# Side-by-side activation words: five matmuls per FFN weight tile instead of six

## The reference

```
for i in range(DEPTH):                      # DEPTH = 2
    x = x + 0.5 * _swiglu(_rmsnorm(x, norm_g[i, 0]), ffn_gu[i, 0], ffn_down[i, 0])
    x = x + mixer(_rmsnorm(x, norm_g[i, 1]))
    x = x + 0.5 * _swiglu(_rmsnorm(x, norm_g[i, 2]), ffn_gu[i, 1], ffn_down[i, 1])
return _rmsnorm(x, final_g), states

def _swiglu(x, w_gu, w_down):
    a, b = jnp.split(x @ w_gu, 2, axis=-1)  # 1024 -> 2 x 2816
    return (jax.nn.silu(a) * b) @ w_down    # 2816 -> 1024
```

## Time and profile before

| | |
|---|---|
| device time, median of 3 runs | 2866.24 us (2864.13 to 2870.95) |
| span of the profiled execution | 2867.4 us |
| the profiled execution's own time | not shown beside its span |
| TensorE matmuls busy | 2731.1 us, 95%, 21041 instructions |
| VectorE / ScalarE / GpSimd busy | 1276.3 us, 45% / 796.0 us, 28% / 285.8 us, 10% |
| one gate_up phase after its first tiles | 1414.9 to 1664.9 us, 250.0 us |
| one down phase | 1281.1 to 1409.5 us, 128.4 us |
| mean granted TensorE clock | 0.966 of 2.4 GHz |

### The profile page before, as it was taken

One profiled execution on the slowest core, in us unless ns is written; L12 is line 12 of the kernel. 1 busy time (PEld: TensorE's weight loads), 2 busy tenths in 40 slices (PEclk: granted clock), 3 DMA queues, 4 the chain that ended last, 5 costly groups with the idle time before them and its releaser, 6 DMA issues.

```text
span 2867.4 us, 49452 instructions
## 1 busy us (share of the span) xinstructions
PE 2731.1 (95%) x21041; PEld 2598.7 (91%) x21041; DVE 1276.3 (45%) x1563; ACT 796.0 (28%) x935; POOL 285.8 (10%) x299
## 2 busy tenths in 40 slices
PE   7999999999999999999999999899889888999997
PEld 6999997989888899999999999788878887999997
DVE  5444233435353454432344423565546654544323
ACT  3222222223231442222322222332223222322222
POOL 1000010101010110000100001003410242100000
PEclk9999999999999999999999999998989898999999
DMA  4333233515152333323433323220012100233231
GB/s 119 88 88 89 82 110 107 166 61 186 60 173 75 125 89 88 97 76 91 114 89 88 83 81 100 77 76 16 30 65 70 51 30 19 74 88 88 84 91 61
DMA packets 340931, 246.85 MB, mean 86 GB/s; under 512 B 9501, under 2 KB 322005, under 8 KB 340801
## 3 DMA queue, kind: packets, MB, share of 16 engines
q1 hardware_dynamic: 326480, 197.32, 23.5%
q0 software_dynamic: 14320, 47.61, 5.1%
HBM read 218.84 MB, written 26.05 MB: 85 GB/s over the span
## 4 chain that ended last, share of the span: by engine, by line
PE 88%; DVE 7%; issue 3%; ACT 2%; DMA 0%; SPq 0%; POOLq 0%; POOL 0%; DVEq 0%; ACTq 0%
PE ps L673 57%; PE ps L850 13%; PE ps L1010 6%; PE ps L771 2%; PE ps L743 1%; DVE cv L1678 1%; PE ps L761 1%; ACT wh L1150 1%; PE ps L749 1%; PE ps L710 1%; DVE wl L1401 1%; PE ps L961 1%; PE ps L968 0%; PE ps L1064 0%; PE ps L973 0%
## 5 line engine op out<-in xcount | busy, mean ns | idle before, releaser
L1401 DVE TENSOR_TENSOR wl<-raw,wh 128x2048 fp32r<-128x2048 f32 (+1 forms) x204 | 427.6, 2096 | 403.3 <-ACT wh L1150 403.3
L673 PE MATMUL ps<-xh,wh 128*128 128x260 f32 x2816 | 569.6, 283 | 4.7 <-DVE gate L1851 4.5
L673 PE MATMUL ps<-xh,wl 128*128 128x260 f32 x2816 | 568.7, 284 | 0.0
L673 PE MATMUL ps<-xl,wh 128*128 128x260 f32 x2816 | 567.9, 283 | 0.0
L1150 ACT ACTIVATE wh<-raw 128x2048 fp32r<-128x2048 f32 (+1 forms) x204 | 354.3, 1737 | 356.8 <-PE ps L673 223.2
L673 PEld LDWEIGHTS ps<-xh,wh 128*128 128x128 f32 x2816 | 436.0, 189 | 6.3 <-issue 5.2
L673 PEld LDWEIGHTS ps<-xh,wl 128*128 128x128 f32 x2816 | 435.5, 189 | 0.0
L673 PEld LDWEIGHTS ps<-xl,wh 128*128 128x128 f32 x2816 | 434.3, 189 | 0.0
L673 PE MATMUL ps<-hh,wh 128*128 128x260 f32 x1408 | 286.9, 285 | 13.4 <-DVE hl L1856 13.4
L673 PE MATMUL ps<-hh,wl 128*128 128x260 f32 x1408 | 284.9, 284 | 0.0
L673 PE MATMUL ps<-hl,wh 128*128 128x260 f32 x1408 | 284.8, 284 | 0.0
(11 more groups left out here) (315 smaller groups left out, 3047.7 us busy)
## 6 DMA issues: line engine op xcount, KB each, us to landing
raw<-in_ffn_gu_dram SPq DMA_DIRECT2D x176, 512.0 KB, 4.9
raw<-in_ffn_down_dram SPq DMA_DIRECT2D x64, 384.0 KB, 3.5
raw<-in_ret_w_in_dram SPq DMA_DIRECT2D x48, 512.0 KB, 4.3
raw<-in_ffn_down_dram SPq DMA_DIRECT2D x64, 320.0 KB, 4.0
s_ring<-in_state_ret_dram POOLq DMA_DIRECT2D x32, 512.0 KB, 4.5
out_dram<-s_ring POOLq DMA_DIRECT2D x32, 512.0 KB, 5.0
raw<-in_gdn_w_in_dram SPq DMA_DIRECT2D x32, 512.0 KB, 4.8
raw<-in_ret_w_out_dram SPq DMA_DIRECT2D x16, 512.0 KB, 4.3
```

The costliest lines, as they stand in the source:

```text
L673: m_ = nc.tensor.matmul(ps[:, 2 * q + h, 0:HALF], w_, v[:, kt0 + t, h * HALF:(h + 1) * HALF], start=b_, stop=e_)
L1401: nc.vector.tensor_tensor(wl[:, s, 0:cols], raw[:, s, 0:cols], wh[:, s, 0:cols].bitcast(F32), ALU.subtract).then_inc(w_low, 1)
```

## The change

In the FFN phases the high and low activation words of a tile lie side by side in one row of 2 x 520 words: first half's 260 high words and its first 86 low words (346), the same for the second half (346), then the remaining 174 low words of both halves (348). A high weight tile then takes three matmuls of 346, 346 and 348 columns; a low one two of 260 as before, on the high words. The low products no longer fall on the columns of the high ones: 2 x 86 columns lie beside them in the unit's two banks, and 348 in a third bank, 4 + u % 2. So evacuation has to add two parts.

- gate_up: ScalarE copies the low part out of PSUM into sq (two copies), VectorE adds it to the main part (this frees the unit) and then multiplies by rinv. The low words of h are written in two pieces.
- down: x gets the main part and then the low part in two pieces.
- The x tiles for gate_up phases (norms 0, 2, 3, 5) have the wide layout, made in two low pieces; those for the mixers and for the last norm stay as they were, in the same memory.
- Start: the sample tokens' transposes stand ahead of the loop, in bank 5, with one copy; the prompt's use banks 6 and 7.

```diff
 SLOT = 16 * P
+LA = 86
+LB = HALF - LA
+WA = HALF + LA
+WIDE = (0, 2, 3, 5)
 
 
...
+        xh = xm[:, 0:KT * NTOK].rearrange("p (t n) -> p t n", t=KT)
+        xl = xm[:, KT * NTOK:2 * KT * NTOK].rearrange("p (t n) -> p t n", t=KT)
+        xw = xm[:].rearrange("p (t n) -> p t n", t=KT)
+
+        def wide_high(tile):
+            return tile[:, 0:2 * WA].rearrange("p (h t) -> p h t", h=2)[:, :, 0:HALF]
+
+        def wide_low(tile):
+            return (tile[:, 0:2 * WA].rearrange("p (h t) -> p h t", h=2)[:, :, HALF:WA],
+                    tile[:, 2 * WA:2 * NTOK].rearrange("p (h t) -> p h t", h=2))
+
+        def pair_low(u):
+            return (ps[:, 2 * (u % 2):2 * (u % 2) + 2, HALF:WA],
+                    ps[:, 4 + u % 2, 0:2 * LB].rearrange("p (h t) -> p h t", h=2))
+
+        def tokens_low(ap):
+            t = halves(ap)
+            return t[:, :, 0:LA], t[:, :, LA:HALF]
...
+                nc.tensor.transpose(ps[:, 5, t * DEC:(t + 1) * DEC], xin_s[:, t * P:(t + 1) * P], ident[0:DEC, 0:DEC])
+            for t in range(KT):
                 if t >= 2:
                     pe.wait_ge(acc_free, t - 1)
-                b = 4 + 2 * (t % 2)
                 if t == 1:
                     pe.wait_ge(gains_ready, 1)
                 for c in range(4):
-                    nc.tensor.transpose(ps[:, b, c * P:(c + 1) * P], xin[:, c, t * P:(t + 1) * P], ident[:])
-                nc.tensor.transpose(ps[:, b + 1, 0:DEC], xin_s[:, t * P:(t + 1) * P],
-                                    ident[0:DEC, 0:DEC]).then_inc(parts_done, 1)
+                    m_ = nc.tensor.transpose(ps[:, 6 + t % 2, c * P:(c + 1) * P], xin[:, c, t * P:(t + 1) * P], ident[:])
+                m_.then_inc(parts_done, 1)
...
+            def wide_products(q, s, n_tiles, col0, tiles, kt0, first, last_):
+
+                for t in range(n_tiles):
+                    c = col0 + t * P
+                    hi_w, lo_w, v = wh[:, s, c:c + P], wl[:, s, c:c + P], tiles[:, kt0 + t]
+                    begin, end = first and t == 0, last_ and t == n_tiles - 1
+                    for h in range(2):
+                        nc.tensor.matmul(ps[:, 2 * q + h, 0:WA], hi_w, v[:, h * WA:(h + 1) * WA], start=begin, stop=False)
+                    nc.tensor.matmul(ps[:, 4 + q, 0:2 * LB], hi_w, v[:, 2 * WA:2 * NTOK], start=begin, stop=end)
+                    for h in range(2):
+                        m_ = nc.tensor.matmul(ps[:, 2 * q + h, 0:HALF], lo_w, v[:, h * WA:h * WA + HALF], start=False, stop=end)
                 return m_
...
-                                        m_ = products(g, s, 1, g * KT * P + t * P, P, xh, xl, t, t == 0, t == KT - 1)
+                                        m_ = wide_products(g, s, 1, g * KT * P + t * P, xw, t, t == 0, t == KT - 1)
...
-                                m_ = products(q, s, 11, 0, P, hh, hl, 11 * s, s == 0, s == 1)
+                                m_ = wide_products(q, s, 11, 0, hw, 11 * s, s == 0, s == 1)
...
-                            act.wait_ge(acc_free, ph.unit0 + 2 * j + 1)
-                            nc.scalar.activation(gate[:], gate[:], ACT.Silu).then_inc(gate_ready, 1)
+                            for g in range(2):
+                                act.wait_ge(parts_done, ph.unit_done(ph.unit0 + 2 * j + g))
+                                low = tokens_low(sq[:, g, :])
+                                nc.scalar.activation(low[0], pair_low(g)[0], ACT.Copy)
+                                nc.scalar.activation(low[1], pair_low(g)[1], ACT.Copy).then_inc(low_moved, 1)
+                                if g == 0:
+                                    act.wait_ge(gu_scaled, 2 * n + 1)
+                                    nc.scalar.activation(gate[:], gate[:], ACT.Silu).then_inc(gate_ready, 1)
                             act.wait_ge(h_ready, n + 1)
                             act.sem_inc(act_held, 1)
-                            nc.scalar.activation(hh[:, j, :], up[:], ACT.Copy).then_inc(h_high, 1)
+                            nc.scalar.activation(wide_high(hw[:, j]), halves(up[:]), ACT.Copy).then_inc(h_high, 1)
                     rolled(act, ph.slots // 2, body, True)
...
+                            high = wide_high(xw[:, t]) if ph.norm in WIDE else halves(xh[:, t, :])
+                            nc.scalar.activation(high, halves(x[:, t, :]), ACT.Copy,
...
+                gain = gains[:, bass.ds(KT * m + t, 1)]
+                if m not in WIDE:
+                    nc.vector.scalar_tensor_tensor(xl[:, t, :], x[:, t, :], gain, xh[:, t, :].bitcast(F32),
+                                                   ALU.mult, ALU.subtract).then_inc(x_low, 1)
+                    return
+                high, low, mine = wide_high(xw[:, t]).bitcast(F32), wide_low(xw[:, t]), tokens_low(x[:, t, :])
+                nc.vector.scalar_tensor_tensor(low[0], mine[0], gain, high[:, :, 0:LA], ALU.mult, ALU.subtract)
+                nc.vector.scalar_tensor_tensor(low[1], mine[1], gain, high[:, :, LA:HALF], ALU.mult, ALU.subtract).then_inc(x_low, 1)
...
-                                dve.wait_ge(parts_done, ph.unit_done(ph.unit0 + 2 * j + g))
-                                nc.vector.tensor_tensor(halves(t_[:]), pair(g), halves(rinv[:]), ALU.mult).then_inc(acc_free, 1)
+                                dve.wait_ge(low_moved, 2 * n + g + 1)
+                                nc.vector.tensor_tensor(halves(t_[:]), pair(g), halves(sq[:, g, :]), ALU.add).then_inc(acc_free, 1)
+                                dve.wait_ge(acc_free, ph.unit0 + 2 * j + g + 1)
+                                nc.vector.tensor_tensor(t_[:], t_[:], rinv[:], ALU.mult).then_inc(gu_scaled, 1)
                             dve.wait_ge(gate_ready, n + 1)
-                            dve.wait_ge(acc_free, ph.unit0 + 2 * j + 2)
+                            dve.wait_ge(gu_scaled, 2 * n + 2)
                             nc.vector.tensor_tensor(up[:], up[:], gate[:], ALU.mult).then_inc(h_ready, 1)
                             dve.wait_ge(h_high, n + 1)
-                            nc.vector.tensor_tensor(hl[:, j, :], up[:], hh[:, j, :].bitcast(F32), ALU.subtract).then_inc(h_low, 1)
+                            high, low, mine = wide_high(hw[:, j]).bitcast(F32), wide_low(hw[:, j]), tokens_low(up[:])
+                            nc.vector.tensor_tensor(low[0], mine[0], high[:, :, 0:LA], ALU.subtract)
+                            nc.vector.tensor_tensor(low[1], mine[1], high[:, :, LA:HALF], ALU.subtract).then_inc(h_low, 1)
...
-                            xt = halves(x[:, t, :])
-                            m_ = nc.vector.scalar_tensor_tensor(xt, pair(q), 0.5, xt, ALU.mult, ALU.add)
-                            m_.then_inc(acc_free, 1)
+                            xt, low, mine = halves(x[:, t, :]), pair_low(q), tokens_low(x[:, t, :])
+                            nc.vector.scalar_tensor_tensor(xt, pair(q), 0.5, xt, ALU.mult, ALU.add).then_inc(x_main, 1)
+                            dve.wait_ge(x_main, KT * ph.index + t + 1)
+                            nc.vector.scalar_tensor_tensor(mine[0], low[0], 0.5, mine[0], ALU.mult, ALU.add)
+                            nc.vector.scalar_tensor_tensor(mine[1], low[1], 0.5, mine[1], ALU.mult, ALU.add).then_inc(acc_free, 1)
```

More of the change, by code:

```diff
@@ L220, in build @@
         x = sb("x", [P, KT, NTOK])
[L221 to L222 removed]
+        xm = sb("xm", [P, 2 * KT * NTOK], F32R)
         raw = sb("raw", [P, 2, SLOT])
@@ L1114, in body @@
                                 pe.wait_ge(acc_free, u - 1)
-                                m_ = products(g, s, KT, g * KT * P, P, xh, xl, 0, True, True)
+                                m_ = wide_products(g, s, KT, g * KT * P, xw, 0, True, True)
                                 m_.then_inc(parts_done, 1)
@@ L1155, in scaled @@
                     act.wait_ge(acc_free, t + 1)
-                nc.scalar.activation(xh[:, t, :], x[:, t, :], ACT.Copy, scale=gains[:, KT * m + t:KT * m + t + 1]).then_inc(x_high, 1)
+                nc.scalar.activation(wide_high(xw[:, t]), halves(x[:, t, :]), ACT.Copy, scale=gains[:, KT * m + t:KT * m + t + 1])\
+                    .then_inc(x_high, 1)
                 if m or t >= 2:
```

19 lines of the change are left out of this document (8 added, 11 removed).

## The result

The changed kernel takes 2894.94 us (median of 4 runs, 2892.43 to 2897.51), the kernel before in the same rounds 2865.18 (2863.83 to 2870.95): ratio 1.0092, 95% interval 1.0076 to 1.0109. It is 0.9% slower, where the prediction said 2853. Its profiled execution took 2895.56 us and spans 2894.0.

What follows compares the result with a forecast made beforehand. TensorE's queue was taken to bound the kernel, busy for 95% of the span. Terms -25.1 + 6.8 + 2.3 + 0.1 + 0.9 + 2.0 = -13.0 us gave 2854.4 in the profile, 2853 us as median; range 2800 to 2877.

Steps and rivals of the forecast that it cites:

- Products: FFN matmuls, five per weight tile instead of six: 11.9 ns saved in each of 2112 tiles, -25.1 us.
- the bounds: Limits set for the saving in the FFN products: 0 and -84.3 us.
- the rate limit: Rival: FFN fp32r columns are fetched at 0.462 ns each, so wide matmuls save nothing; 2878 us, chance 0.13.
- gate_up to down: TensorE's wait for the last h tile, four times: added evacuation steps, about 1.7 us each, +6.8 us (4 to 10).
- First slot: First slot of a gate_up: copies add 0.75 us before TensorE's awaited evacuation, in three of four FFNs, +2.3 us.
- down: x in three steps instead of one: +0.1 us going into the next phase, +0.9 us behind the last unit.
- Clock: More time lost to low clock after the longer gate_up-to-down gaps: +2 us (0 to +7).
- Start: Kernel start: one PSUM copy less per tile, other transpose banks, against split low pieces: 0 us (-2 to +1).
- 2.7 ns per matmul: Rival: in FFN products only 2.7 ns go with each matmul, the rest per column; saves 5.7 us, 2873 us, chance 0.11.
- loads bind: Rival: weight loads make the FFN matmuls' 120 ns, and longer matmuls are free of it; -83.0 us, 2795 us, chance 0.13.

Runs made afterwards that it cites:

- e9: TensorE alone, no model: fp32r matmuls of single sizes, then whole weight tiles; a tile of six takes 720.6 ns, one of five 713.5, however split.
- e11: TensorE alone, tiles given the kernel's conditions one by one; with moving rows walking 1040 words apart, the change's tile goes from 713.8 to 721.3 ns.
- e13: Changed kernel with rows of 1056 words instead of 1040 and blocks starting at 0, 352 and 704: ratio 1.0024 to the kernel before.
- e2: Changed kernel with the old evacuation, the low part in PSUM never read: 2876.66 us against 2870.64 for the kernel before, ratio 1.0025.
- e1: TensorE alone, 96 matmuls of one form per block, varying columns, weight width and fp32r or bf16: fp32r 119.6 ns at 260 columns, 159.2 at 346.
- e5: TensorE alone, blocks of 64 fp32r matmuls, moving operand starting at different word offsets: 260 columns took 118.4 to 124.1 ns, 346 took 156.7 to 160.0.
- e12: TensorE alone, tiles walking over rows with only row distance or block starts changed: the change's tile takes 721.9 ns at 1040 words, 713.1 at 1152.

## Why the prediction was wrong

By its own steps, in us of the profiled executions (2854.4 forecast, 2894.0 measured, 39.6 between):

1. *Products*, -25.1 forecast. Measured: 1408 tiles of gate_up at 721.5 for 720.6 ns, and 704 of down about 0.3 ns longer with half of their low clock taken off, **+1.5**. This step failed, and it is 26.6 of the 39.6 us. It failed twice. Its reason, a fixed share that goes with each matmul, was right in kind but not in size: a tile of five alone takes 713.5 for 720.6 (e9), which is 7, not 11.9 ns, since what remains over the columns grows from 11.8 to 12.7 ns for each matmul; at the first starts of e11 it is only 2.5. And those 7 ns exist only for some starts of the moving blocks. Both ends of the bounds were from counts and columns (the far one is given as -84.3, and its working comes to -83.0); where the blocks lie, which the change also moves, was not priced at all. The 42 ns between the 346 and 260 columns' means looks like the rate limit's 40, and the stretch of 242 us too, but the rate limit is refuted: e13 changes no column and gets 713.2.
2. *gate_up to down*, +6.8: four gaps of 5.15 for 3.65, **+6.0**. Right.
3. *First slot*, +2.3: 1.24 for 0.56 us, three times, **+2.1**. Right.
4. *down*, +0.1 and +0.9: behind the last unit the norm sum starts 4.66 us after the last matmul for 3.85, **+0.8**, as said. The +0.1 was wrong: the prediction looked for the cover at the norm sum, but TensorE meets the late x step earlier, at the next phase's second unit, which waits for its banks: 1.15 for 0.35 us at three places, **+2.4**.
5. *Clock*, +2: in the four FFNs 25.8 us at the low clock for 20.4, half of the difference lost, **+2.7**. The end behind the last norm sum has 13.8 us for 12.0, another **+0.9**; e2, with the old evacuation, has the same. Against the second trace of before (6.8 us in the FFNs) the 2.7 would be 9.5, so this term's size hangs on the execution one compares with. Over the whole span the two traces differ by 20.8 us of low clock, 10.4 us of time: the term looked only behind the gaps, while 6.8 of the 10.4 lie in the mixers.
6. *Start*, 0: 39.0 us for 38.0, **+0.9**; but the second trace of before has 39.2, so this is not shown to be the change's.

Terms 1 to 5 come to 16.4, where the FFN column shows 15.7 (1583.6 - 1567.9); half of the low clock is a rough price. The other 10.0 us are the mixers, +5.2 and +4.7, where the forecast had nothing. 6.8 of them are half of the low clock that these two traces have more there (47.8 for 44.4 and 126.3 for 116.1 us), and executions of one kernel differ by as much. The 3 us that are left lie in the first mixer, in the changed kernel's two traces and in e2. Their cause stays open: in the four traces of wide kernels with the old order of waits TensorE goes 1.0 to 1.8 us from one matmul's start to the next at two places of the first mixer (in the changed kernel at 727.2 and 880.5) with nothing that it waits for, and in no trace of the others. That is 2.2 to 3.1 us a kernel. The kernels with the moved wait also have a longer program on TensorE, so the order of waits need not be the reason. I did not test it.

The rivals: the rate limit would have given 2878 and came nearest, for the wrong reason; "2.7 ns per matmul" is too little for e9 (7 ns) and for e13 against the kernel before (713.2 for 720.6 ns), about right at the first starts of e11 (2.5 ns), and gave the changed kernel nothing, so it is no price per matmul either; "loads bind" is refuted by the 32-column weights (118.4 ns for 119.6). The range ended at 2877, and what lay beyond it, no saving at all with a late entry and slower mixers, had been given no room.

## What to carry to other kernels

A fixed cost per matmul that is read from one shape is a sum of things; before it is priced by count, look at what else the merging moves, here the starts and the row distance of the moving operand, and time the exact tile with the exact layout by itself. When steps are added behind a product, follow them to each place where TensorE takes the bank back, also in the next phase, and ask first whether the wait on the path is needed so early: moving one wait gave 18 to 20 us, more than the products can give (15). Compare stages between fixed marks with two traces of the same kernel at hand, since a stage outside the change can wander by 15 us, and take the low clock off before reading the difference: here it explained all but 3 of the mixers' 10 us.

## What the hardware showed that was not expected

- From 256 columns on, fp32r matmuls of 128x128 weights have 10 to 19 ns over columns/2.4 GHz (e1, e5, e9), bf16 ones 3 to 4 (e1: 260 columns 10.73 us over 96, 111.8 ns; 346 columns 148.2). The Trainium skill (TensorE: Matmul & The Clock Gate, Back-to-back issue gap) has N/2.4 + 2.5; the bf16 runs come near it, the fp32r runs do not.
- The same tile of five fp32r matmuls takes 713.1 to 713.8 or up to 721.9 ns by nothing but where its moving blocks start in SBUF (e12). One tile in the walk takes from 705 to 733 ns, the same again for the same row (705 and 705, 732 and 733, in e11).
- Five splits of the same 1560 columns into five matmuls all take 713.3 to 713.8 ns (e9), though single sizes in a row do not add up to that.
